# RWKV's triangular inverse on its 64x64 diagonal blocks, and the recurrence's last products grouped by rows

## The reference

```
def step(state, inp):                                   # 4 heads of 64, over 256 positions
    r_t, w_t, k_t, v_t, kk_t, a_t = inp
    sa = einsum('bhvk,bhk->bhv', state, -kk_t)
    state = state * w_t + sa (x) (kk_t * a_t) + v_t (x) k_t
    return state, einsum('bhvk,bhk->bhv', state, r_t)
_, y = lax.scan(step, zeros, xs)
```

## Time and profile before

| | us |
|---|---|
| median of 3 runs | 1754.03 (1751.93 to 1755.36) |
| the profiled execution | 1752.18 |
| its span in the profile | 1750.4 |
| TensorE busy | 1656.7 (95% of the span) |
| VectorE busy | 618.9 (35%) |
| ScalarE busy | 446.2 (25%) |
| GpSimd busy | 28.2 (2%) |
| mean granted clock of TensorE | 0.976 |

### The profile page before, as it was taken

The page is one execution under the profiler, slowest core; times in us unless marked ns, Lnnn a source line. Parts: engine busy times, 40 slices in busy tenths (PEclk is TensorE's granted clock), DMA queues, the critical chain, the costliest instruction groups (busy, mean ns, idle before and its releaser), DMA issues.

```text
span 1750.4 us, 33961 instructions
## 1 busy us (share of the span) xinstructions
PE 1656.7 (95%) x15082; PEld 1118.6 (64%) x15082; DVE 618.9 (35%) x1008; ACT 446.2 (25%) x681; POOL 28.2 (2%) x17
## 2 busy tenths in 40 slices
PE   6999989899998999999979999999999999899995
PEld 6977768699987987768655643456336653356421
DVE  4657783655553567694530010100100001010101
ACT  4544422444443544532310000000100000000000
POOL 0000020000000000020000000000000000000000
PEclk9989999999998989999989999999999999999999
DMA  7423402444663522421389999999999999999995
GB/s 271 169 73 132 153 29 73 144 172 173 221 217 134 192 97 81 160 73 49 139 356 418 361 398 422 420 419 419 421 422 419 419 420 421 421 419 419 420 422 220
DMA packets 65298, 472.90 MB, mean 270 GB/s; under 512 B 7232, under 2 KB 7232, under 8 KB 8320
## 3 DMA queue, kind: packets, MB, share of 16 engines
q1 hardware_dynamic: 64784, 469.07, 67.2%
q0 software_dynamic: 368, 1.65, 0.2%
HBM read 469.64 MB, written 1.05 MB: 269 GB/s over the span
## 4 chain that ended last, share of the span: by engine, by line
PE 76%; DVE 9%; SPq 5%; DMA 5%; ACT 2%; issue 2%; DVEq 0%; ACTq 0%
PE bank L562 63%; SPq L524 5%; DMA ring_c<-stream 5%; DVE arena L1624 3%; DVE ring_a_r L1624 1%; PE bank L1156 1%; PE bank L923 1%; DVE xn L1624 1%; PE bank L1211 1%; DVE arena L1630 1%; ACT high_a L1304 1%; PE bank L916 1%; PE bank L780 1%; PE bank L838 1%; PE bank L1170 1%
## 5 line engine op out<-in xcount | busy, mean ns | idle before, releaser
L562 PE MATMUL bank<-ring_c,hsel 128*32 128x256 f32 (+1 forms) x3312 | 289.6, 420 | 5.3 <-DMA ring_c<-stream 5.3
L1624 DVE TENSOR_TENSOR ring_a_r<-ring_a,high_a 128x2048 fp32r<-128x2048 f32 x82 | 187.3, 2290 | 135.6 <-ACT high_a L1304 135.5
L1624 DVE TENSOR_TENSOR arena<-arena,bank 128x256 f32<-128x256 f32 (+2 forms) x122 | 54.1, 471 | 506.4 <-ACT arena L1557 472.4
L562 PEld LDWEIGHTS bank<-ring_c,hsel 128*32 128x32 f32 (+1 forms) x3312 | 129.8, 115 | 153.2 <-issue 87.2
L1304 ACT ACTIVATE high_a<-ring_a 128x2048 fp32r<-128x2048 f32 x82 | 156.9, 1914 | 130.5 <-PE bank L562 111.5
L1557 ACT ACTIVATE arena<-bank 128x256 f32<-128x256 f32 (+1 forms) x84 | 26.2, 346 | 568.7 <-PE bank L562 568.7
L562 PE MATMUL bank<-hT_h,ring_a_r 128*128 128x256 f32 (+1 forms) x592 | 168.0, 284 | 0.0
L562 PE MATMUL bank<-high_a,hT_h 128*128 128x512 f32 (+1 forms) x416 | 164.6, 396 | 0.8 <-issue 0.8
L562 PE MATMUL bank<-high_a,hT_l 128*128 128x512 f32 (+1 forms) x416 | 159.6, 384 | 0.0
L562 PE MATMUL bank<-ring_a_r,hT_h 128*128 128x512 f32 (+1 forms) x416 | 159.5, 384 | 0.0
L562 PE MATMUL bank<-ring_a,hsel 128*32 128x256 f32 (+1 forms) x2104 | 148.1, 398 | 0.4 <-DVE hsel L1624 0.4
(11 more groups left out here) (313 smaller groups left out, 1982.3 us busy)
## 6 DMA issues: line engine op xcount, KB each, us to landing
ring_a<-stream SPq DMA_DIRECT2D x207, 1024.0 KB, 6.9
ring_c<-stream SPq DMA_DIRECT2D x196, 1024.0 KB, 26.5
ring_b<-stream SPq DMA_DIRECT2D x40, 1024.0 KB, 26.1
consts<-const SPq DMA_DIRECT2D x1, 1272.0 KB, 7.7
resid<-x SPq DMA_DIRECT2D x1, 1024.0 KB, 5.1
y<-xn SPq DMA_DIRECT2D x2, 512.0 KB, 2.6
smalls<-small SPq DMA_DIRECT2D x1, 824.5 KB, 11.3
smalls<-small POOLq DMA_DIRECT2D x1, 824.5 KB, 7.4
```

The lines of the kernel that those rows point to most:

```text
L562: ins = mm(o, lhsT, rhs, start=start, stop=stop)
L1624: return v.tensor_tensor(o, i0, i1, op)
```

## The change

The eight 128x128 matrices of the inverse are kept as their diagonal blocks only: the block of rows 0-63 in partitions 0-63 and that of rows 64-127 in partitions 64-127, both 64 columns wide, side by side for the eight matrices in 512 columns instead of 1024. Each product becomes two, one for each block (CHUNKS), on the rows and columns 0-63 and 64-127 of TensorE, both into the same bank. The copies and additions of an episode take 256 columns instead of 512. The masked products of VectorE and GpSimd take one instruction for each block, 64 partitions and 8x64 elements. The transposes for X become products with the identity. The constant "level" has 384 columns instead of 768. rw_app multiplies each block with its rows of [A | LkV] (128 columns). In rw_Y all products over 128 rows come first, heads in turn, then all those over 64 rows; only the first product of the bank carries start.

```diff
@@ -202,7 +202,7 @@
     return out, at
 
 CONST, N_CONST = _columns([("ident", 128), ("pair_ones", 128), ("pair_mean", 128), ("negtri", 128), ("masks", 256),
-                           ("level", 768), ("ident64", 64), ("reset", 256), ("ones", 256), ("before", 128),
+                           ("level", 384), ("ident64", 64), ("reset", 256), ("ones", 256), ("before", 128),
                            ("iota", 256), ("pick", 8), ("key", 8), ("place_rank", 8), ("holds", 8), ("over_from", OVERS), ("eps", 1), ("gn_eps", 1), ("one", 1), ("is_f", 1), ("is_i", 1)])
 SMALL, N_SMALL = _columns([("w_uq", 512), ("w_qidx", 256), ("w_uv", 256), ("wa_up", 256), ("g_up", 256), ("router", 64),
                            ("g_mix", 8), ("g_ffn", 8), ("mu", 8), ("w0", 2), ("a0", 2), ("k_k", 2), ("k_a", 2), ("r_k", 2),
@@ -224,7 +224,8 @@
     put("negtri", np.where(j <= i, 0.0, NEG))
     chunk = i // 64 == j // 64
     put("masks", np.concatenate([(i < j) & chunk, (i <= j) & chunk], 1))
-    put("level", np.concatenate([(i < j) & (i // 2 ** (n + 1) == j // 2 ** (n + 1)) & (i // 2 ** n != j // 2 ** n)
+    ic, jc = i % 64, np.arange(64)[None, :]
+    put("level", np.concatenate([(ic < jc) & (ic // 2 ** (n + 1) == jc // 2 ** (n + 1)) & (ic // 2 ** n != jc // 2 ** n)
                                  for n in range(6)], 1))
     put("ident64", (i % 64) == np.arange(64)[None, :])
     put("reset", (np.arange(256) % 64 != 0)[None, :])
@@ -427,7 +428,10 @@
     S2, S3 = (Zf[:, 512 + 128 * n:640 + 128 * n].rearrange("p (a b) -> p a b", a=2) for n in range(2))
     ALV, XALV = lev[:, 0, :, :], lev[:, 1, :, :]
     Zm = area(8, T)
-    XT = Zm.rearrange("p a b -> p (a b)")[:, 0:8 * P].rearrange("p (a b) -> p a b", a=8)
+
+    XT = Zm.rearrange("p a b -> p (a b)")[:, 0:512].rearrange("p (a b) -> p a b", a=8)
+    Xd, Zd = (w[:, 0:512].rearrange("p (a b) -> p a b", a=8) for w in (Xf, Zf))
+    levd = [lev[:, n, :, :].rearrange("p a b -> p (a b)")[:, 0:512].rearrange("p (a b) -> p a b", a=8) for n in range(2)]
     bon = area(2, T)
     Ys, Yc, Yq = Wf, t0, cml
     rwkv_top = top[0]
@@ -482,6 +486,7 @@
     def filled(name):
         return sem(f"bank{EP_BANK[name]}_full")
 
+    CHUNKS = (slice(0, 64), slice(64, 128))
     HEADS = [(h, h // 2, slice(64 * (h % 2), 64 * (h % 2) + 64)) for h in range(4)]
 
     def tsl(tt):
@@ -900,7 +905,8 @@
             for i in range(2):
                 begin(pe, l, f"rX0_{i}")
                 for j in range(4):
-                    ins = nc.tensor.transpose(bank(f"rX0_{i}")[:, j * P:j * P + P], XT[:, 4 * i + j, :], ident)
+                    for cs in CHUNKS:
+                        ins = mm(bank(f"rX0_{i}")[cs, j * 64:j * 64 + 64], XT[cs, 4 * i + j, :], ident[cs, cs], start=True, stop=True)
                 ins.then_inc(filled(f"rX0_{i}"), 1)
 
         def rw_merge(l, j):
@@ -913,14 +919,16 @@
                 ep = f"rZ{j}_{i}"
                 begin(pe, l, ep)
                 for q in range(4 * i, 4 * i + 4):
-                    ins = mm(bank(ep)[:, (q % 4) * P:(q % 4) * P + P], lev[:, j % 2, q, :], X[:, q, :], start=True, stop=True)
+                    for cs in CHUNKS:
+                        ins = mm(bank(ep)[cs, (q % 4) * 64:(q % 4) * 64 + 64], levd[j % 2][cs, q, :], Xd[cs, q, :], start=True, stop=True)
                 ins.then_inc(filled(ep), 1)
             for i in range(2):
                 drained(pe, l, f"rZ{j}_{i}")
-                for ep, lhs, rhs in ((f"rX{j}_{i}", XT, Z), (f"rT{j}_{i}", Z, XT))[j == 5:]:
+                for ep, lhs, rhs in ((f"rX{j}_{i}", XT, Zd), (f"rT{j}_{i}", Zd, XT))[j == 5:]:
                     begin(pe, l, ep)
                     for q in range(4 * i, 4 * i + 4):
-                        ins = mm(bank(ep)[:, (q % 4) * P:(q % 4) * P + P], lhs[:, q, :], rhs[:, q, :], start=True, stop=True)
+                        for cs in CHUNKS:
+                            ins = mm(bank(ep)[cs, (q % 4) * 64:(q % 4) * 64 + 64], lhs[cs, q, :], rhs[cs, q, :], start=True, stop=True)
                     ins.then_inc(filled(ep), 1)
 
         def rw_app(l):
@@ -939,7 +947,8 @@
                 drained(pe, l, f"rT5_{i}")
                 begin(pe, l, f"rXA{i}")
                 for q in range(4 * i, 4 * i + 4):
-                    ins = mm(bank(f"rXA{i}")[:, (q % 4) * P:(q % 4) * P + P], XT[:, q, :], ALV[:, q, :], start=True, stop=True)
+                    for cs in CHUNKS:
+                        ins = mm(bank(f"rXA{i}")[cs, (q % 4) * P:(q % 4) * P + P], XT[cs, q, :], ALV[cs, q, :], start=True, stop=True)
                 ins.then_inc(filled(f"rXA{i}"), 1)
 
         def rw_state(l):
@@ -991,17 +1000,19 @@
             drained(pe, l, "rS3")
             begin(pe, l, "rY")
             entering = {1: lambda blk: GW[:, 0, blk, 0, :], 2: lambda blk: S2[:, blk, :], 3: lambda blk: S3[:, blk, :]}
-            for h, blk, ps in HEADS:
+
+            for blk in range(2):
                 for tt in range(TT):
-                    q = 2 * h + tt
-                    o = bank2("rY")[ps, blk, tsl(tt)]
-                    mm(o, XALV[:, q, 64:128], LQ[:, h, tt, P:2 * P], start=True, stop=False)
-                    mm(o, Vtm[:, tt, h * 64:h * 64 + 64], KQ[:, h, tt, P:2 * P], start=False, stop=False)
-                    for c in range(2):
-                        n = 2 * tt + c
-                        if n:
-                            ins = mm(bank2("rY")[ps, blk, n * 64:n * 64 + 64], entering[n](blk)[ps, :],
-                                     RpT[ps, blk, n * 64:n * 64 + 64], start=False, stop=c == 1)
+                    for h, _, ps in HEADS[2 * blk:2 * blk + 2]:
+                        mm(bank2("rY")[ps, blk, tsl(tt)], XALV[:, 2 * h + tt, 64:128], LQ[:, h, tt, P:2 * P],
+                           start=blk == 0 and tt == 0, stop=False)
+                    for h, _, ps in HEADS[2 * blk:2 * blk + 2]:
+                        mm(bank2("rY")[ps, blk, tsl(tt)], Vtm[:, tt, h * 64:h * 64 + 64], KQ[:, h, tt, P:2 * P], start=False, stop=False)
+            for blk in range(2):
+                for n in range(1, 4):
+                    for h, _, ps in HEADS[2 * blk:2 * blk + 2]:
+                        ins = mm(bank2("rY")[ps, blk, n * 64:n * 64 + 64], entering[n](blk)[ps, :],
+                                 RpT[ps, blk, n * 64:n * 64 + 64], start=False, stop=blk == 1 and n == 3)
             ins.then_inc(filled("rY"), 1)
 
         def rw_gn(l):
@@ -1481,12 +1492,12 @@
             elif s == "rw_x0":
                 for i in range(2):
                     full(act_e, l, f"rX0_{i}")
-                    a(X[:, 4 * i:4 * i + 4, :].rearrange("p a b -> p (a b)"), bank(f"rX0_{i}")[:, :], ACT.Copy).then_inc(freed(f"rX0_{i}"), 1)
+                    a(Xd[:, 4 * i:4 * i + 4, :].rearrange("p a b -> p (a b)"), bank(f"rX0_{i}")[:, 0:256], ACT.Copy).then_inc(freed(f"rX0_{i}"), 1)
             elif s[:4] == "rw_m" and s[4:].isdigit():
                 j = int(s[4])
                 for i in range(2):
                     full(act_e, l, f"rZ{j}_{i}")
-                    a(Z[:, 4 * i:4 * i + 4, :].rearrange("p a b -> p (a b)"), bank(f"rZ{j}_{i}")[:, :], ACT.Copy).then_inc(freed(f"rZ{j}_{i}"), 1)
+                    a(Zd[:, 4 * i:4 * i + 4, :].rearrange("p a b -> p (a b)"), bank(f"rZ{j}_{i}")[:, 0:256], ACT.Copy).then_inc(freed(f"rZ{j}_{i}"), 1)
             elif s == "rw_app":
                 full(act_e, l, "rLkV")
                 a(ALV[:, :, 64:128], bank("rLkV")[:, :].rearrange("p (q v) -> p q v", q=8), ACT.Copy).then_inc(freed("rLkV"), 1)
@@ -1926,8 +1937,10 @@
                 drained(ve, l, "rLT3")
                 lt = LQ.rearrange("p h t n -> p (h t) n")[:, :, 0:P]
                 lvl = c_("level").rearrange("p (a b) -> p a b", a=6)
-                link(tt_(XT, lt, lvl[:, 0:1, :].broadcast_to([P, 8, P]), ALU.mult))
-                tt_(XT, XT, c_("ident").unsqueeze(1).broadcast_to([P, 8, P]), ALU.add).then_inc(sem("rw_xt0"), 1)
+                for cs in CHUNKS:
+                    ins = tt_(XT[cs, :, :], lt[cs, :, cs], lvl[cs, 0:1, :].broadcast_to([64, 8, 64]), ALU.mult)
+                link(ins)
+                tt_(XT, XT, c_("ident64").unsqueeze(1).broadcast_to([P, 8, 64]), ALU.add).then_inc(sem("rw_xt0"), 1)
             elif s == "rw_app":
                 drained(ve, l, "rtA")
                 v.tensor_copy(ALV[:, :, 0:64].rearrange("p (h t) d -> p h t d", t=TT),
@@ -1938,10 +1951,10 @@
             elif s[:4] == "rw_m" and s[4:].isdigit():
                 j = int(s[4])
                 for i in range(2):
-                    for ep, dst in ((f"rX{j}_{i}", X), (f"rT{j}_{i}", XT))[j == 5:]:
+                    for ep, dst in ((f"rX{j}_{i}", Xd), (f"rT{j}_{i}", XT))[j == 5:]:
                         full(ve, l, ep)
                         d3 = dst[:, 4 * i:4 * i + 4, :]
-                        tt_(d3, d3, bank2(ep, P), ALU.add).then_inc(freed(ep), 1)
+                        tt_(d3, d3, bank(ep)[:, 0:256].rearrange("p (a b) -> p a b", a=4), ALU.add).then_inc(freed(ep), 1)
```

(5 more changed lines are left out.)

## The result

The changed kernel takes 1724.63 us (median of 5, 1722.80 to 1726.80) against 1754.75 in the same runs before (median of 5, 1751.93 to 1756.78): ratio 0.983, with 95% interval 0.9817 to 0.9839, or 28.3 to 32.1 us. Forecast were 27.8 us and a time of 1726. The profiled execution is the one of 1724.63, its span 1722.8 against 1750.4: 27.6 us less.

A forecast was written before the change was run, and what follows sets the result against it. Bound by waits on TensorE's products and VectorE's element-wise work, then the experts' DMA stream from 875 us. Gains of 13.7 us a layer, twice, plus 0.4 for constants make 27.8: 1726 us, main case 1719 to 1733, range 1719 to 1741.

The forecast's parts named there:

- The path: From 875 us the experts' stream keeps its length; microseconds gained in layers 0 and 1 arrive at the end.
- The pace of a pass: TensorE's new 64x64 passes in the inverse: 0.027 us each, so 32 take 0.86 us where 16 old took 1.86.
- rivals 3 and 4: 3: chunks sharing a bank run one after another, 1742 us, chance 0.10; 4: tile changes drain the array, 1782, 0.04.
- level 4: Inverse level on TensorE at full clock: 3.15 us instead of 5.63, 2.5 us gained a layer.
- VectorE's stretch: 226 to 255 us in layer 0, where TensorE waits for VectorE: 2.9 us gained a layer.
- (a): XT at the start of the inverse, VectorE's addition behind GpSimd's products: 1.0 us gained, bounds 0.4 to 1.5.
- (b, c): VectorE's splits, then additions beside GpSimd in branches 1 and 2: no change, bounds -1.2 to +1.2 us for each addition.
- rival 2: A GpSimd instruction on 64 partitions costs as much as one on 128, so VectorE waits longer: 1740 us, chance 0.09.
- rival 1: The clock stays at the lower level through the inverse's levels 3 to 5, 0.054 us a pass: 1735 us, chance 0.12.
- level 3: Inverse level after TensorE's idle stretch, 3.4 us at half speed: 4.65 us instead of 7.2, 2.55 gained a layer.
- The application: Products applying the inverse (L942), 32 passes of 128 columns plus tile-size changes: 0.1 us lost a layer.
- rY: Last products of the recurrence, grouped by row count: 2.9 us instead of 7.12, 4.25 gained a layer, bounds 3 to 4.6.

The follow-up runs named there:

- the two halves of the change: Changed kernel with the old product order in rY: 1739.84 us, ratio 0.991; kernel before with only rY's grouped order: 1750.53 us, ratio 0.9971.

## Why the prediction was right

**The path.** Right. The stream behind 875 us kept its length to 0.4 us in the profile of the result, and what was gained in the two layers arrived at the end. In the second execution the stream was 2.8 us longer, so its length is not a constant.

**The pace of a pass.** Forecast 0.027 us, measured 0.029: a record of 64 is 2.08 us and one of 32 is 1.15, so (2.08 - 1.15) / 32. This was the step on which rivals 3 and 4 hung. The experiment without the second chunk shows that its products overlap almost wholly with the first chunk's, though both write one bank. In the changed kernel's trace the passes of the two tiles start in pairs, 0.007 us apart, with a pair every 0.058; 64 columns of a gate product take 0.029 (0.234 for 512), so the two passes of a pair don't merely take turns. So the rule of the Trainium skill that I had weighed (TensorEngine Tiling (Array Packing), "Gotcha 1: PSUM Pressure") does not hold for this form, in which the two tiles write different partitions of the bank. The rest of the period of level 4 (3.39, forecast 3.15) is 0.74 to X's first addition instead of 0.70, 0.15 instead of 0.05 from the freed bank to the next Z, and 0.05 for ScalarE.

**VectorE's stretch.** The sum, 3.8 us, was forecast 2.9, and its terms were off in both directions. (a) The third of the three instructions still stood behind GpSimd's four pieces, which end at 229.5 and took 5.95, not 5.66; 0.25 us gained instead of 1.0, less than my lower bound. (b, c) 1.5 us gained where I took none: a wait of VectorE behind GpSimd lasts until the end of the piece under way, and the pieces are half as long. The later start of GpSimd showed that this is the cause. I had used this very argument in (a), where it failed, and not in (c), where it holds. The trace shows what is different in (a). VectorE's three instructions there take 0.99, 1.66 and 1.64 us; in the kernel with the copies behind gate21, where GpSimd comes later, the first two take 0.68 and 0.69. So in (a) all three have two operands in SBUF and stand one behind another, and some 2.2 us are lost in three waits where the kernel before lost about 2 in one. In branch 1 each such instruction is followed by one out of PSUM, which doesn't wait (0.69). There the shorter piece is a gain, while in (a) one instruction more waits. No run tests this by itself.

**GpSimd (rival 2).** Two halves cost 2.60 us where nothing runs beside them, the one before 2.36. 512 elements on 64 partitions cost 1.30, and on 128 partitions 1.27: the elements of a partition count. By the rule of the Trainium skill which I cited (GPSIMD Engine Reference, 2.1 Instruction dispatch) two half products cost what the one did, and the trace agrees to a tenth (2.60 against 2.36).

**The clock (rival 1).** Half of it happened: level 3 had the lower level throughout, 4.8 us of work and not 3.4, so it gained 2.06 and not 2.55. Levels 4 and 5 had the full clock, which is what the rival denied. In a second execution of the same kernel it was 4.60 us for level 3, so this term is not one number.

**The application.** -0.45 instead of -0.1. Its 32 passes took 1.89 until the next product against 1.70, and each of the three pieces of full-size products around it 0.07 to 0.10 more. I had counted two changes of tile size, 0.26, and taken 0.16 off for passes that run two at a time; that saving did not come.

**rY.** Forecast 2.9, measured 2.75; so the price of 0.13 a change, worked out from 16 of them, fits. The step has two parts that no run separates: fewer changes (about 2.0 us), and passes over 128 rows that alternate between the two column tiles, 32 of them in 1.90 us with the change behind them, where they took 0.12 each before. I had counted one change in the new order, and by the count of 16 it is two, as there is one more behind rY.

**What was luck.** Too little in (c), too much in (a), level 3, level 4 and the application cancel to 0.2 us a layer. And a larger error didn't show: I took for granted that the rest of the kernel keeps its clock. In the changed kernel's first profile it did (84.6 us against 84.8), in its second not quite (90.5). In the two halves of the change it did not, and by the same reckoning their times were forecast 6.4 and 3.7 us too low. No part of the prediction gives a reason why it should hold for the whole and not for the halves. The range, built from the mechanisms' bounds, held no term for that.

**Open.** What decides where the stretches of lower clock fall in the gate and output products. They repeat partly with a kernel (0.83 twice in 850 to 920 us, in two executions) and differ partly between its executions. Moving work by some us moves them, and I found no row that would have told it ahead. A test would shift the start of the recurrence by a few tenths at a time and count; it wasn't made.

## What to carry to other kernels

Pack block-diagonal matrices as tiles of TensorE's rows and columns and issue them in turn: the second block was then free here, and in blocks of four the level took a fifth longer. Group small products by the number of rows. Where VectorE and GpSimd both read SBUF, cut the work of GpSimd into pieces: VectorE waits for the piece under way. It helps where VectorE's instructions with two SBUF operands alternate with others (1.5 us in branch 1), and did little where they follow one another (0.25 us at XT). And put independent products into an idle stretch ahead of a chain that waits on its own results, not behind it: here it spared both the idle time and the low clock in the chain, though only half of that reached the end. Compare small changes by the length of the changed stretch in the profiles as well as by the total, and look at the pace of the first products too.

## What the runs showed of the hardware that was not expected

Less work can be slower: without the second chunk's products, TensorE stayed at 1.2 GHz for 23.9 us instead of 6.8 in each layer, and the two recurrences took 14.4 us more. The time at the lower level is 80 to 105 us in the profiles of all kernels with full work, whatever was done to the recurrence, so a gain of a few us in steps can halve in the total: 8.7 became 5.0, 7.8 became 3.7. The start is one such place: TensorE's first products went at half pace until 15.8 to 17.3 us in ten of the profiled executions and until 21 to 23 in four, 1.6 to 2.2 us of time, where the view shows a granted clock of 1.00 throughout. An addition of two SBUF operands on VectorE that meets GpSimd takes 0.92 to 1.60 us beside pieces of 64x512 and up to 2.76 beside one of 128x1024, where it takes 0.69 alone; the instructions of the branches that read PSUM kept 0.68 to 0.69.
